# Two engines that stop waiting for their own last instruction, and a 3-tap convolution over two features in turn

## The chip, the cores and the metric

The kernel runs on one core of a Trainium2 chip. Its time is the device time of one execution in microseconds (us), lower is better; 2675.78 us is the median of three executions before the change. The engines named here are TensorE (PE; its weight loads are listed apart as PEld), VectorE (DVE), ScalarE (ACT), GpSimd (POOL) and SyncE (SP), which issues the loads of the weights. Each engine runs its own instructions in order; across engines, and also behind an engine's own earlier instructions, order is kept only by semaphores that an instruction raises when it ends and that another waits for.

## What is computed

One transformer-like block ("block 1") and then two layers of a second kind, on 256 tokens of width 1024, all in fp32. Cut to what matters:

```python
# block 1
h = rms_norm(x) * (1 + scale) + shift;  z = h @ w_in
o = swa_attention(...), rg_lru(conv4(xr)) * gelu(yr), moba_attention(...)     # three branches
x = x + gate * ((sigmoid(g) * (o @ w_branch)).sum() @ w_out)
u = conv3(rms_norm(x) @ w_up);  x = x + gate * ((silu(u_gate) * u_val) @ w_down)   # conv3: 3 taps, per feature
# two layers, each: half FFN, mixer, cross attention to a memory, half FFN
x = x + 0.5 * norm((silu(h @ w1) * (h @ w3)) @ w2)
x = x + norm(merge(conv31(glu), differential attention, pooling) @ w_out)
x = x + norm(cross_attention(x, mem) @ w_o)
```

## The kernel before, in words

Activations lie in SBUF with features on the 128 partitions and the 256 tokens along the free axis, so a feature tile is 128x256 and there are eight of them. Every matrix product runs in fp32 accuracy out of three products of rounded parts: each operand is split into a rounded part ("hi") and the rest ("lo"), and TensorE adds hi*hi, lo*hi and hi*lo. Weights stream from HBM in 704 *units* of up to 512 rows by 256 columns, through six raw buffers. For each unit ScalarE rounds the weights (`hi`, L1099, output `weights_hi`) and VectorE subtracts to get the rest (`lo`, L1421, output `weights_lo`), into a ring of four, three units ahead of TensorE (`pe_unit`, L842). `hi` waits until TensorE has finished the unit that used its ring place before.

The activations are split in the same way: `act_split` (L1170) writes the rounded tile (`h_hi`, `gh`, `mh`), `vec_split` (L1555, L1558) the rest (`h_lo`, `gl`, `ml`). TensorE waits for the split of each feature tile that it reads.

All engines walk one common list of steps, written by `plan`. `spread` mixes chains of small steps (attention heads, the recurrence, the 31-tap convolution) among the gemm units. Steps that the change and the prediction speak of:

- `enter`: four pairs of tiles, each residual add (`vec_residual`, L1574 and L1576, or L1569 in block 1's form), two `act_split`, two `vec_split` and a square (`act_square`, L1144). Between two stages nothing else is there for TensorE.
- attention heads: `pe_scores`, `vec_softmax` (row maxima L1618), `act_softmax` (four exponentials L1218, each followed by a read of the accumulator), `vec_softmax` again (scaling of the probabilities, L1646 and L1648 for the differential form, L1655 otherwise), `pe_turn`, `act_turn` (L1228), `pe_pv`, `vec_pv` (L1664).
- the 31-tap convolution of the mixers: half of the features on VectorE (`vec_conv31`, L1844, three taps a step), half on ScalarE and GpSimd (products `prod` L1359, sums L1973).
- the 3-tap convolution of block 1 (`act_up1`, `vec_up1`): ScalarE writes the last tap of two features, VectorE adds the other two taps of each (L1805).

In the kernel before, nearly every ScalarE and VectorE instruction is followed by a wait of the same engine for that instruction's own semaphore. Only the products L1359 have none. The waits look like this one, in `lo`:

```python
dve.tensor_tensor(WL[s], RAWB[...], WH[s], ALU.subtract).then_inc(sems["weights_rest"], 1)
dve.wait_ge(sems["weights_rest"], up("weights_rest", ("rest", m)))
```

`up` counts the raises of a semaphore and notes the value at which a named result is ready, for the engines that wait for it.

Of the kernel before, what the change touches and what calls it, by code (L numbers as in the profile page):

```python
# [23 lines left out]
P = 128  # L24
# [12 lines left out]
FFN_K = 3  # L37
# [518 lines left out]
def build(nc, a, out, scratch, marks, final, stop=None):  # L556
# [530 lines left out]
    def _(act):  # L1087
# [3 lines left out]
        def hi(m):  # L1091
# [8 lines left out]
            act.wait_ge(sems["weights_rounded"], up("weights_rounded", ("rounded", m)))  # L1100

        def rstd(dst, src, scale, eps, sem, name, s):
# [3 lines left out]
            act.wait_ge(sems[sem], up(sem, name))  # L1106
# [32 lines left out]
        def act_square(k):  # L1139
            p = k["p"]  # L1140
# [5 lines left out]
            act.wait_ge(sems["act_norm"], up("act_norm", ("sq", k["key"], p)))  # L1146
# [6 lines left out]
        def act_adapt(k):  # L1153
            for f in range(NF):
# [4 lines left out]
                act.wait_ge(sems["act_split"], up("act_split", ("split_hi", "H", k["key"], f)))  # L1159

        def act_split(k):
            h = xbuf(k["buf"], k["gen"])[0]
            f = k["f"]
# [7 lines left out]
            act.wait_ge(sems["act_split"], up("act_split", ("split_hi", k["buf"], k["gen"], k["ft0"] + f)))  # L1171

        def act_evac_y(k):
            act.wait_ge(sems["gemm_done"], at("unit", k["last_unit"]))
            ft = k["ft"]
            if k["sq"] is None:
                act.copy(Y[:, ft:ft + 2, :], slot(k["id"])).then_inc(sems["act_drain"], 1)
                act.wait_ge(sems["act_drain"], up("act_drain", ("evac", k["id"])))
# [3 lines left out]
            act.wait_ge(sems["act_drain"], up("act_drain", ("sqy", k["sq"], ft // 2)))  # L1182
            for i in range(2):
                act.activation(Y[:, ft + i, :], slot(k["id"])[:, i, :], ACT.Copy,
                               scale=col(k["gain"][0], k["gain"][1] + ft + i)).then_inc(sems["act_drain"], 1)
                act.wait_ge(sems["act_drain"], up("act_drain", ("evac", k["id"])))
            mark(("y", k["yk"], ft // 2), "act_drain")

        def act_evac_qk(k):
# [5 lines left out]
            act.wait_ge(sems["act_drain"], up("act_drain"))  # L1195
# [9 lines left out]
        def act_evac_v1(k):  # L1205
            act.wait_ge(sems["gemm_done"], at("unit", k["last_unit"]))
            act.copy(BUF[k["dst"]][:, :, k["c0"]:k["c0"] + k["cols"]], GP[:, k["id"] % 2, :, 0:k["cols"]]).then_inc(sems["act_drain"], 1)
            act.wait_ge(sems["act_drain"], up("act_drain", ("evac", k["id"])))
            mark(("tm", k["dst"], 0), "act_drain")

        def act_softmax(k):
            c = att(k["cfg"], k["i"])
            act.wait_ge(sems["vec_attn"], at("max", k["cfg"], k["i"]))
            for qt in range(2):
                nk = P * (qt + 1) if c["causal"] else T
                for m in range(c["maps"]):
                    j = 2 * qt + m
                    act.activation(c["E"][:, qt, m, 0:nk], scores_at(c, qt, m, nk), ACT.Exp, bias=NM[:, j:j + 1], accum_out=DEN[:, j:j + 1]).then_inc(sems["act_attn"], 1)  # L1218
                    act.wait_ge(sems["act_attn"], up("act_attn", ("exps", k["cfg"], k["i"])))
            if k["cfg"] == "swa":  # L1220
                act.activation(ES[:], ES[:], ACT.Exp).then_inc(sems["act_attn"], 1)
                act.wait_ge(sems["act_attn"], up("act_attn", ("sink_exp", k["cfg"], k["i"])))

        def act_turn(k):
# [4 lines left out]
            act.wait_ge(sems["act_attn"], up("act_attn", ("pt", k["cfg"], k["i"], m)))  # L1229

        def act_pv(k):
            if k["cfg"][:4] == "diff":
                act.wait_ge(sems["pe_attn"], at("o_ps", k["cfg"], k["i"]))
                act.activation(ASQ[:, k["i"] // 2 % 2, k["i"] % 2, :], PV[:, 0:T], ACT.Square).then_inc(sems["act_attn"], 1)
                act.wait_ge(sems["act_attn"], up("act_attn", ("o_sq", k["cfg"], k["i"])))
# [8 lines left out]
        def act_evac_xr(k):  # L1244
# [3 lines left out]
            act.wait_ge(sems["act_drain"], up("act_drain", ("evac", k["id"])))  # L1248
            mark(("xr", k["ft"]), "act_drain")

        def act_evac_yr(k):
# [3 lines left out]
            act.wait_ge(sems["act_drain"], up("act_drain"))  # L1255
            act.activation(SQ[:, s, :], slot(k["id"]), ACT.Square).then_inc(sems["act_drain"], 1)
            act.wait_ge(sems["act_drain"], up("act_drain", ("evac", k["id"])))

        def act_gelu(k):
# [3 lines left out]
            act.wait_ge(sems["act_gelu"], up("act_gelu", ("gelu_tanh", k["ft"])))  # L1263

        def act_rnn_gate(k):
# [5 lines left out]
            for g in range(2):  # L1271
                act.activation(o_b1["rg"][:, f % 2, g, :], STAT[:, g * T:(g + 1) * T], ACT.Tanh, scale=0.5,
                               bias=HALFB[:, 8 * g + f:8 * g + f + 1]).then_inc(sems["act_rnn"], 1)
                act.wait_ge(sems["act_rnn"], up("act_rnn", ("stat_read", k["s"])))
            mark(("gate_tanh", "rnn", f), "act_rnn")

        def act_rnn_in(k):
# [4 lines left out]
            act.wait_ge(sems["act_rnn"], up("act_rnn"))  # L1282
# [782 lines left out]
```

## Time and profile before

| | |
|---|---|
| median of three executions | 2675.78 us (2674.79 to 2678.45) |
| the profiled execution, first to last instruction | 2675.4 us |
| TensorE busy | 2407.3 us (90%) |
| VectorE busy | 1800.0 us (67%) |
| ScalarE busy | 1431.5 us (54%) |
| GpSimd busy | 375.0 us (14%) |
| mean granted TensorE clock | 0.942 of full speed |

The profile is one execution; its span agrees with the median within 0.4 us, so sums are made against the span. A busy TensorE is not one at its full pace: the granted clock has two levels, 1.2 and 2.4 GHz, shown as 0.5 and 1.0.

### The profile page before, as it was taken

How to read it: one execution, taken by the hardware profiler on the slowest of the kernel's cores; microseconds unless marked ns; L12 is line 12 of the kernel's file. 1: busy time of each engine (PE TensorE's matmuls, PEld its weight loads, DVE VectorE, ACT ScalarE, POOL GpSimd, SP SyncE). 2: the span in 40 equal slices, each digit the busy share in tenths (PEclk: the TensorE clock that was granted, in tenths of full speed). 3: DMA queues.
4: the chain of work that ended last, by engine and by line, in shares of the span. 5: the costliest groups of instructions: out<-in, count | busy, mean ns of one | idle time of the engine just before them, and what ended most of it. 6: DMA issues, size and time to landing. Idle time of an engine off the chain costs nothing. (4 is left out here: it accounts for less than half of the span.)

```text
span 2675.4 us, 45893 instructions
## 1 busy us (share of the span) xinstructions
PE 2407.3 (90%) x18041; PEld 2291.6 (86%) x18041; DVE 1800.0 (67%) x2425; ACT 1431.5 (54%) x2074; POOL 375.0 (14%) x354
## 2 busy tenths in 40 slices
PE   5988798999998998989898998998998988898997
PEld 5976797999998987878797998998987888797997
DVE  5666886996764886877455664664896877454663
ACT  2564445764445645665635445545644765635443
POOL 1000000110010553420000100010453430000010
PEclk7998998999999998999899999999998999899999
DMA  8534474556654552335343654654452335253652
GB/s 249 147 97 125 149 227 143 175 187 215 182 180 143 157 170 69 118 113 172 104 148 105 189 180 141 175 180 150 143 176 70 115 118 177 94 159 95 189 177 84
DMA packets 402055, 400.52 MB, mean 150 GB/s; under 512 B 18006, under 2 KB 399304, under 8 KB 401841
## 3 DMA queue, kind: packets, MB, share of 16 engines
q1 hardware_dynamic: 399457, 389.27, 47.8%
q0 software_dynamic: 2384, 8.32, 1.1%
q8 instruction: 144, 2.36, 0.4%
q14 instruction: 70, 0.57, 0.1%
HBM read 396.45 MB, written 1.09 MB: 149 GB/s over the span
## 5 line engine op out<-in xcount | busy, mean ns | idle before, releaser
L1421 DVE TENSOR_TENSOR weights_lo<-raw_weights,weights_hi 128x1024 fp32r<-128x1024 f32 x704 | 871.7, 1238 | 471.1 <-ACT weights_hi L1099 457.3
L842 PE MATMUL gemm_ps<-h_hi,weights_hi 128*128 128x256 f32 x3664 | 1074.6, 293 | 98.7 <-DVE h_lo L1555 58.0
L1099 ACT CAST weights_hi<-raw_weights 128x1024 fp32r<-128x1024 f32 x704 | 727.7, 1034 | 617.5 <-PE gemm_ps L842 559.8
L842 PE MATMUL gemm_ps<-h_lo,weights_hi 128*128 128x256 f32 x3664 | 1053.1, 287 | 0.0
L842 PE MATMUL gemm_ps<-h_hi,weights_lo 128*128 128x256 f32 x3664 | 1052.5, 287 | 0.0
L842 PEld LDWEIGHTS gemm_ps<-h_hi,weights_hi 128*128 128x128 f32 x3664 | 720.5, 197 | 115.8 <-issue 89.3
L842 PEld LDWEIGHTS gemm_ps<-h_lo,weights_hi 128*128 128x128 f32 x3664 | 720.8, 197 | 4.1 <-issue 3.0
L842 PEld LDWEIGHTS gemm_ps<-h_hi,weights_lo 128*128 128x128 f32 x3664 | 719.8, 196 | 0.0
L1973 POOL TENSOR_TENSOR y<-y,prod 128x256 f32<-128x256 f32 x240 | 237.3, 989 | 393.5 <-ACT prod L1359 209.8
L1961 POOL TENSOR_TENSOR hidl<-hf,hidh 128x512 fp32r<-128x512 f32 x55 | 73.8, 1342 | 1344.2 <-ACT hidh L1343 1344.2
L842 PE MATMUL gemm_ps<-hidh,weights_hi 128*128 128x256 f32 x880 | 248.2, 282 | 2.0 <-DVE weights_lo L1421 2.0
L842 PE MATMUL gemm_ps<-hidh,weights_lo 128*128 128x256 f32 x880 | 245.7, 279 | 0.0
L842 PE MATMUL gemm_ps<-hidl,weights_hi 128*128 128x256 f32 x880 | 245.5, 279 | 0.0
L842 PE MATMUL gemm_ps<-gh,weights_hi 128*128 128x256 f32 x544 | 165.3, 304 | 34.8 <-DVE gl L1558 19.9
L1844 DVE SCALAR_TENSOR_TENSOR y<-zp,param_cols,y 128x256 f32<-128x256 f32 x240 | 170.2, 709 | 8.5
L842 PEld LDWEIGHTS gemm_ps<-hidh,weights_hi 128*128 128x128 f32 x880 | 165.2, 188 | 2.4 <-DVE weights_lo L1421 2.2
L842 PEld LDWEIGHTS gemm_ps<-hidh,weights_lo 128*128 128x128 f32 x880 | 165.4, 188 | 0.0
L842 PEld LDWEIGHTS gemm_ps<-hidl,weights_hi 128*128 128x128 f32 x880 | 164.7, 187 | 0.2
L842 PE MATMUL gemm_ps<-gl,weights_hi 128*128 128x256 f32 x544 | 157.4, 289 | 0.0
L842 PE MATMUL gemm_ps<-gh,weights_lo 128*128 128x256 f32 x544 | 157.2, 289 | 0.0
L842 PEld LDWEIGHTS gemm_ps<-gh,weights_hi 128*128 128x128 f32 x544 | 108.6, 200 | 39.9 <-issue 32.5
L842 PEld LDWEIGHTS gemm_ps<-gl,weights_hi 128*128 128x128 f32 x544 | 108.4, 199 | 1.4 <-issue 1.0
(282 smaller groups left out, 2926.7 us busy)
## 6 DMA issues: line engine op xcount, KB each, us to landing
raw_weights<-in_ffn_w_dram SPq DMA_DIRECT2D x256, 512.0 KB, 3.9
raw_weights<-in_w_in_dram SPq DMA_DIRECT2D x200, 512.0 KB, 3.8
raw_weights<-in_w_mod_dram SPq DMA_DIRECT2D x48, 512.0 KB, 4.9
raw_weights<-in_w_up_dram SPq DMA_DIRECT2D x44, 512.0 KB, 4.0
raw_weights<-in_xattn_kv_dram SPq DMA_DIRECT2D x32, 512.0 KB, 3.8
raw_weights<-in_w_out_dram SPq DMA_DIRECT2D x24, 512.0 KB, 3.9
raw_weights<-in_w_down_dram SPq DMA_DIRECT2D x20, 512.0 KB, 4.4
raw_weights<-in_w_branch_dram SPq DMA_DIRECT2D x16, 512.0 KB, 4.3
```

The costliest lines, as they stand in the source:

```text
L842: mm = pe.matmul(ps[:, c, 0:T], w[:, m, kt, c * P:(c + 1) * P], x[:, f, :], start=start, stop=stop_)
L1099: act.copy(WH[s], RAWB[:, u["raw"] % RAW, 0:u["nkt"], 0:u["cols"]]).then_inc(sems["weights_rounded"], 1)
L1421: dve.tensor_tensor(WL[s], RAWB[:, u["raw"] % RAW, 0:u["nkt"], 0:u["cols"]], WH[s], ALU.subtract).then_inc(sems["weights_rest"], 1)
L1844: dve.scalar_tensor_tensor(out=Y[:, f, :], in0=o_m["zp"][:, f, j:j + T], scalar=col(f"dw{l}", 8 * j + f), in1=Y[:, f, :], op0=ALU.mult, op ...
L1961: pool.tensor_tensor(l_[:, s, :], src, h[:, s, :], ALU.subtract).then_inc(sems["hidden_rest"], 1)
L1973: pool.tensor_tensor(Y[:, f, :], Y[:, f, :], o_m["prod"][:, b, i, :], ALU.add).then_inc(sems["pool_conv"], 1)
```

## The change

At 69 places the wait of ScalarE or VectorE for its own last instruction is taken out; the raise of the semaphore stays, so other engines wait as before. Where the result is read by the next instruction of the same engine, the wait stays or is set just ahead of the reader. Several waits are put in for readers further on (`vec_qk_norm`, `vec_subln`, `vec_softmax`, `vec_evac_branch`). Two orders are changed: the differential softmax scales the second map of both query tiles before it combines either, and the 3-tap convolution runs tap by tap over two features instead of feature by feature. `vec_conv31`, `vec_mod`, `vec_rnn_conv`, `vec_rnn_mult`, `vec_rnn_scan` and the set-up keep their waits. No instruction that computes is added, removed or changed in size. The core of the diff (the places left out replace `wait_ge(sems[s], up(s, name))` by `up(s, name)` in the same way):

```diff
         def hi(m):
...
             act.copy(WH[s], RAWB[:, u["raw"] % RAW, 0:u["nkt"], 0:u["cols"]]).then_inc(sems["weights_rounded"], 1)
-            act.wait_ge(sems["weights_rounded"], up("weights_rounded", ("rounded", m)))
+            up("weights_rounded", ("rounded", m))
...
         def act_split(k):
...
-            act.wait_ge(sems["act_split"], up("act_split", ("split_hi", k["buf"], k["gen"], k["ft0"] + f)))
+            up("act_split", ("split_hi", k["buf"], k["gen"], k["ft0"] + f))
...
         def act_softmax(k):
...
                     act.activation(c["E"][:, qt, m, 0:nk], scores_at(c, qt, m, nk), ACT.Exp, bias=NM[:, j:j + 1], accum_out=DEN[:, j:j + 1]).then_inc(sems["act_attn"], 1)
-                    act.wait_ge(sems["act_attn"], up("act_attn", ("exps", k["cfg"], k["i"])))
+                    up("act_attn", ("exps", k["cfg"], k["i"]))
...
         def lo(m):
...
-            dve.wait_ge(sems["weights_rest"], up("weights_rest", ("rest", m)))
+            up("weights_rest", ("rest", m))
...
         def vec_split(k):
...
-            dve.wait_ge(sems["vec_split"], up("vec_split", ("split", k["buf"], k["gen"], d)))
+            up("vec_split", ("split", k["buf"], k["gen"], d))
...
         def vec_softmax(k):
...
+                second = []
                 for qt in range(2):
                     nk = P * (qt + 1)
                     dve.tensor_scalar(E[:, qt, 1, 0:nk], E[:, qt, 1, 0:nk], RD[:, 2 * qt + 1:2 * qt + 2], None, ALU.mult).then_inc(sems["vec_attn"], 1)
-                    dve.wait_ge(sems["vec_attn"], up("vec_attn"))
+                    second.append(up("vec_attn"))
+                for qt in range(2):
+                    nk = P * (qt + 1)
+                    dve.wait_ge(sems["vec_attn"], second[qt])
                     dve.scalar_tensor_tensor(out=E[:, qt, 0, 0:nk], in0=E[:, qt, 0, 0:nk], scalar=RD[:, 2 * qt:2 * qt + 1], in1=E[:, qt, 1, 0:nk], op0=ALU.mult, op1=ALU.add).then_inc(sems["vec_attn"], 1)
-                    dve.wait_ge(sems["vec_attn"], up("vec_attn", ("probs", k["cfg"], k["i"])))
+                    up("vec_attn", ("probs", k["cfg"], k["i"]))
...
         def vec_up1(k):
...
-            for i in range(2):
-                f = 22 * v + 2 * j + i
-                for n in range(FFN_K - 1):
+            tap = [None, None]
+            for n in range(FFN_K - 1):
+                for i in range(2):
+                    f = 22 * v + 2 * j + i
+                    if n:
+                        dve.wait_ge(sems["vec_ffn"], tap[i])
                     dve.scalar_tensor_tensor(out=uc[:, v, i, :], in0=raw_up[:, v, i, n:n + T],
                                              scalar=col("ffn_conv_w", 44 * n + f), in1=uc[:, v, i, :], op0=ALU.mult,
                                              op1=ALU.add).then_inc(sems["vec_ffn"], 1)
-                    dve.wait_ge(sems["vec_ffn"], up("vec_ffn", ("conv_gate" if v == 0 else "conv_val", j)))
+                    tap[i] = up("vec_ffn", ("conv_gate" if v == 0 else "conv_val", j))
```

## Rows read from the trace of the kernel before

**Rows 1.** The page: busy time by engine; granted TensorE clock in 40 slices.

```profile
PE 2407.3 (90%) x18041; PEld 2291.6 (86%) x18041; DVE 1800.0 (67%) x2425; ACT 1431.5 (54%) x2074; POOL 375.0 (14%) x354
...
PEclk7998998999999998999899999999998999899999
```

**Rows 2.** Waits of TensorE: us in total, times, longest us.

```profile
PE gemm_ps L842 <- DVE h_lo L1555: 58.0, 21, 6.5
...
PE gemm_ps L842 <- DVE gl L1558: 19.9, 2, 10.0
```

**Rows 3.** Waits of the two engines that prepare weights, same columns.

```profile
ACT weights_hi L1099 <- PE gemm_ps L842: 559.8, 359, 4.4
DVE weights_lo L1421 <- ACT weights_hi L1099: 457.3, 328, 7.8
```

**Rows 4.** Stretches: length, busy of PE, PEld, DVE, ACT, POOL, clock, DMA.

```profile
56.00:332.00 276.00, 229.96 (x1559) 204.17 (x1558) 185.13 (x345) 153.75 (x251) 0.89 (x1) 0.91 0.47 137
346.00:413.00 67.00, 63.92 (x536) 62.60 (x535) 58.43 (x93) 33.64 (x50) 0.00 (x0) 1.00 0.77 240
477.00:592.00 115.00, 113.10 (x940) 112.55 (x938) 106.69 (x135) 85.57 (x116) 16.64 (x11) 1.00 0.57 174
668.00:852.00 184.00, 184.00 (x1530) 183.02 (x1528) 109.31 (x110) 88.67 (x102) 14.28 (x11) 1.00 0.60 181
882.00:995.00 113.00, 102.75 (x818) 99.17 (x818) 106.07 (x120) 66.69 (x108) 70.79 (x68) 1.00 0.57 176
1005.00:1175.00 170.00, 144.08 (x949) 127.86 (x949) 135.32 (x200) 113.06 (x216) 69.47 (x69) 0.90 0.31 96
1189.00:1227.00 38.00, 32.77 (x266) 31.78 (x265) 29.21 (x42) 22.77 (x31) 0.00 (x0) 1.00 0.43 133
1264.00:1327.00 63.00, 48.51 (x302) 43.46 (x303) 30.33 (x44) 37.88 (x59) 0.76 (x1) 0.84 0.29 93
```

**Rows 5.** Timeline of ScalarE at 900 us (start, length), and the products' durations in ns.

```profile
899.99 1.05 ACT L1099 CAST weights_hi<-raw_weights 128x1024 fp32r<-128x1024 f32 x1 [1.85 <-PE gemm_ps L842]
901.07 1.31 ACT L1359 ACTIVATE prod<-zp,param_cols 128x256 f32<-128x256 f32 x3
902.29 0.62 ACT L1310 ACTIVATE gt<-gt 128x512 f32<-128x512 f32 x1
...
L1359 ACT ACTIVATE prod<-zp,param_cols x240: 492/498/517, 885.1 to 2174.7; 128x256 f32<-128x256 f32 x120
```

**Rows 6.** Timeline of VectorE in one attention head, and of TensorE behind it.

```profile
1051.73 0.69 DVE L1421 TENSOR_TENSOR weights_lo<-raw_weights,weights_hi 128x512 fp32r<-128x512 f32 x1
1052.46 1.15 DVE L1618 TENSOR_REDUCE neg_max<-misc_ps 128x2 f32<-128x256 f32 x2
1055.96 0.18 DVE L1637 RECIPROCAL rden<-den 128x4 f32<-128x4 f32 x1 [2.35 <-ACT e L1218]
...
1057.53 0.48 DVE L1648 SCALAR_TENSOR_TENSOR e<-e,rden 128x256 f32<-128x256 f32 x1
...
1059.81 0.55 PE L842 MATMUL gemm_ps<-gh,weights_hi 128*128 128x256 f32 x1 [9.99 <-DVE gl L1558]
```

**Rows 7.** Chain that ended last, in an enter: start us, us, what.

```profile
2457.18 0.70 DVE y L1574
...
2458.69 0.52 ACT h_hi L1170
...
2459.30 0.48 DVE h_lo L1555
...
2459.84 0.50 DVE h_lo L1555
...
2460.36 0.70 DVE y L1574
```

**Rows 8.** Groups by line: busy us, mean ns of one, idle before.

```profile
L1844 DVE SCALAR_TENSOR_TENSOR y<-zp,param_cols,y 128x256 f32<-128x256 f32 x240 | 170.2, 709 | 8.5
...
L1555 DVE SCALAR_TENSOR_TENSOR h_lo<-x_res,param_cols,h_hi 128x256 fp32r<-128x256 f32 x64 | 31.0, 484 | 38.3 <-ACT h_hi L1170 36.1 <-DVE h_lo L1555 0.4
```

**Rows 9.** Timeline of VectorE at the 3-tap convolution.

```profile
508.42 1.22 DVE L1421 TENSOR_TENSOR weights_lo<-raw_weights,weights_hi 128x1024 fp32r<-128x1024 f32 x1
509.68 2.05 DVE L1805 SCALAR_TENSOR_TENSOR uc<-up,param_cols,uc 128x256 f32<-128x256 f32 x4
```

More of the change, by code:

```diff
@@ L1105, in rstd @@
             act.activation(dst, dst, ACT.Exp, scale=-0.5).then_inc(sems[sem], 1)
-            act.wait_ge(sems[sem], up(sem, name))
+            up(sem, name)
         def act_setup(k):
@@ L1281, in act_rnn_in @@
             act.activation(o_b1["xr"][:, f, 0:T], s, ACT.Exp, scale=-1.0).then_inc(sems["act_rnn"], 1)
-            act.wait_ge(sems["act_rnn"], up("act_rnn"))
+            up("act_rnn")
             act.activation(o_b1["s_all"][:, f, :], s, ACT.Tanh).then_inc(sems["act_rnn"], 1)
-            act.wait_ge(sems["act_rnn"], up("act_rnn", ("a", f)))
+            up("act_rnn", ("a", f))
         def act_rnn_sqrt(k):
@@ L1545, in vec_adapt @@
                 dve.scalar_tensor_tensor(out=HL[:, f, :], in0=Y[:, f, :], scalar=MODC[:, c:c + 1], in1=HH[:, f, :], op0=ALU.add, op1=ALU.subtract).then_inc(sems["vec_norm"], 1)
-                dve.wait_ge(sems["vec_norm"], up("vec_norm", ("split", "H", k["key"], f)))
+                up("vec_norm", ("split", "H", k["key"], f))
         def vec_split(k):
@@ L1587, in vec_evac_qk @@
             dve.tensor_copy(BUF[k["dst"]][:, k["ft"]:k["ft"] + 2, :], slot(k["id"])).then_inc(sems["vec_drain"], 1)
-            dve.wait_ge(sems["vec_drain"], up("vec_drain", ("evac", k["id"])))
+            up("vec_drain", ("evac", k["id"]))
+            mark(("qk_raw", k["dst"], k["ft"]), "vec_drain")
         def vec_qk_norm(k):
@@ L1622, in vec_softmax @@
                 i = k["i"]
+                dve.wait_ge(sems["vec_attn"], at("max", k["cfg"], k["i"]))
                 for qt in range(2):
@@ L1625, in vec_softmax @@
                     dve.tensor_tensor(NM[:, j], NM[:, j], SINK[:, 2 * i:2 * i + 2], ALU.min).then_inc(sems["vec_attn"], 1)
-                    dve.wait_ge(sems["vec_attn"], up("vec_attn"))
+                    last_min = up("vec_attn")
+                dve.wait_ge(sems["vec_attn"], last_min)
                 for qt in range(2):
@@ L1795, in vec_ffn_val @@
             dve.tensor_tensor(o_f2["hf"][:, b], fa, fb[:], ALU.mult).then_inc(sems["vec_ffn"], 1)
-            dve.wait_ge(sems["vec_ffn"], up("vec_ffn", ("hidden", key, k["j"])))
+            up("vec_ffn", ("hidden", key, k["j"]))
         def vec_up1(k):
@@ L1817, in vec_up1 @@
                                          op0=ALU.mult, op1=ALU.mult).then_inc(sems["vec_ffn"], 1)
-                dve.wait_ge(sems["vec_ffn"], up("vec_ffn", ("hidden", "b1u", j)))
+                up("vec_ffn", ("hidden", "b1u", j))
         def vec_pads2(k):
@@ L1859, in vec_pool_w @@
                 dve.scalar_tensor_tensor(out=o_m["gl2"][:, f, :], in0=slot(k["id"])[:, i, :], scalar=col(f"pscale{l}", f), in1=o_m["gh2"][:, f, :], op0=ALU.mult, op1=ALU.subtract).then_inc(sems["vec_split"], 1)
-                dve.wait_ge(sems["vec_split"], up("vec_split", ("split", "G", f"l{l}mq", f)))
+                up("vec_split", ("split", "G", f"l{l}mq", f))
             mark(("evac", k["id"]), "vec_split")
@@ L1890, in vec_mem_turn @@
                 dve.tensor_copy(o_c["memf"][:, 4 * half:4 * half + 4, :].rearrange("p f t -> p (f t)"), PBF[:, 0:1024]).then_inc(sems["vec_norm"], 1)
-                dve.wait_ge(sems["vec_norm"], up("vec_norm", ("memf", f"l{k['l']}", half)))
+                up("vec_norm", ("memf", f"l{k['l']}", half))
         parts = dict(setup=vec_setup, params=vec_params, turn_x=vec_turn_x, mod=vec_mod, mod_sum=vec_mod_sum, adapt=vec_adapt, split=vec_split,
```

106 lines of the change are left out of this document (54 added, 52 removed).

## The prediction

> **What bounds the kernel now.** I read the page first, then the waits, a table of stretches, and last the timelines of the stretches in which TensorE is idle. TensorE is busy for 2407.3 of 2675.4 us, so 268 us at most lie in its idle time, and its granted clock lies under 0.9 in seven of the 40 slices [rows 1]. It is 1.00 in the stretches where TensorE hardly idles and 0.84 to 0.91 in three of those where it does [rows 4]; what is missing there was granted at the 1.2 GHz level. The waits show for what it is idle: above all for the rests of activations, 58.0 us in 21 waits on one line and 19.9 us in only two on another [rows 2]. The two engines that prepare operands are no bound on average. ScalarE's rounding of weights sat idle 559.8 us until TensorE had freed a ring place, and VectorE's subtraction 457.3 us until the rounding was done [rows 3]: where the weights flow, TensorE sets the pace, and a faster ScalarE or VectorE only waits longer.
>
> The table of stretches separates the two situations. In a feed-forward network TensorE is busy 184.00 of 184 us at the 2.4 GHz level; nothing that the change does can show there. In the mixers, the attention and the merges TensorE lacks 2 to 46 us a stretch, and VectorE is busy for up to 94% (106.07 of 113 us) and 80% (135.32 of 170 us) [rows 4]. There a chain of small VectorE and ScalarE instructions ends last. The gain must come from these chains.
>
> **What one removed wait is worth.** *ScalarE.* The trace has instructions without the wait: three products of 0.498 us each take 1.31 us together instead of 1.49, so each starts 0.09 us before the one ahead has ended, and the tanh behind them, which waits for another engine's finished work, starts at 902.29 while the products run to 902.38. Behind the rounding, which has its own wait, the products start 0.03 us late (901.04 to 901.07) [rows 5]. A removed wait between two ScalarE instructions of which the second is otherwise ready is thus worth 0.09 + 0.03 = 0.12 us.
>
> *VectorE.* Nowhere in this trace do two of its instructions stand without the wait. Known is the gap, 0.04 us (1052.42 to 1052.46), and the fixed part of an instruction: 512 columns take 0.69 us and 1024 take 1.22, so 0.16 us do not depend on the columns [rows 6, 9]. The bounds are 0 (the next one starts no earlier in any case) and 0.16 + 0.035 = 0.19 us (the whole fixed part is hidden). I take 0.11 us, just under ScalarE's value, which is the nearest row.
>
> The Trainium skill's page "VectorE: DVE Perf Modes", section "The DRAIN you can't avoid", speaks against that: each VectorE instruction is followed by a flush, the next cannot start before it, and eight copies took 13.88 us with a semaphore behind each and with one behind the last alone. By that rule the VectorE part of the sum is nothing and the time is that of the first rival below. The section "Two Vector instructions with no wait between them" of the same page says that an instruction whose tensors start in the same partitions as those before it is not held and starts earlier; all tiles here start at partition 0. No row of this trace decides between the two.
>
> **The change part by part.** I followed the chains back along the timelines from each stall of TensorE to the TensorE instruction that had released them, and counted on them the neighbours (gap under 0.06 us) whose wait goes; S is their number on ScalarE, V on VectorE. A stretch cannot gain more than TensorE lacks in it. A wait that stays for a reader costs what it did.
>
> - *Enters* (residual, split). One cycle lasts 3.18 us (2457.18 to 2460.36) and on VectorE holds two freed neighbours: rest to rest, and rest to the next product [rows 7]. Residual to rounding goes over to ScalarE and keeps its price. V = 7 an enter, 0.77 us, seven enters: 5.4 us. Block 1's form has V = 11: 1.2 us. Sum 6.6.
> - *Conv31 with the gated inputs.* Only the weights' rest ahead of three taps, and the gates, are freed; the taps keep their waits. S = 7, V = 42: 5.4 us of 10.2 that TensorE lacks [rows 4]; two layers: 10.9.
> - *Differential attention and the merge behind it.* In the head shown, TensorE idles 9.99 us behind a chain that runs through two maxima, four exponentials, four scalings and the rest [rows 6]. Freed on it: one neighbour of the maxima, three of the exponentials, three of the scalings (their new order leaves each pair independent), four around them. Over the stretch S = 33, V = 67: 11.4 us of 26 [rows 4]; two layers: 22.7.
> - *Last merge of the mixer.* S = 1, V = 29: 3.3 us of 5.2 [rows 4]; two layers: 6.6.
> - *Memory and cross attention.* S = 20, V = 7: 3.2 us of 14.5 [rows 4]; two layers: 6.3.
> - *Block 1.* Up to 332 us S = 51, V = 60: 12.7 us of 46. The merge (346 to 413) and the feed-forward network with the 3-tap convolution (477 to 592) have long chains, but TensorE lacks only 3.1 and 1.9 us there, which is all that they can give [rows 4]. The four taps now take 2.05 us [rows 9]; tap by tap they have three freed neighbours and take about 1.7, at 44 steps behind a TensorE that is busy 98%, so the new order is worth nearly nothing. With 0.9 us in the second adaptive norm: 18.6.
> - *Output.* V = 3: 0.3.
> - *Weights elsewhere, feed-forward networks of the layers, the waits put in for later readers.* Nothing: TensorE covers them [rows 3, 4]; the new waits are for results that are several instructions old. If that cover failed, each would cost a gap of 0.04 us.
>
> Nothing is moved past a DMA queue: SP issues a load when the weights' rest has been taken, as before, and POOL's list is untouched.
>
> The sum is 6.6 + 10.9 + 22.7 + 6.6 + 6.3 + 18.6 + 0.3 = 72 us if nothing else is right behind each chain. Something often is: 376 of 704 rests of weights found their rounding already done, 328 waited for it [rows 3], so close to half of what VectorE gains is met by another wait. Between 0.53 (376/704) and 1 I take 0.65, nearer to the low end because TensorE itself paces the roundings. 72 x 0.65 = 47 us: 2675.4 - 47 = 2628 us, and with the 0.4 us by which the median lies above the span, **2629 us**. Time regained at the 2.4 GHz level is inside the counts, as the lacks include slow matmuls only in part; I add nothing for it.
>
> **Rivals.**
>
> 1. *VectorE regains nothing, ScalarE all of its own.* The S terms alone: in block 1 51 x 0.12 = 6.1, in its merge S = 8 or 1.0, and the 1.9 that its feed-forward network can give; in the layers 7, 33, 1 and 20 neighbours or 0.8 + 4.0 + 0.1 + 2.4, twice; 23.6 us; by 0.65 that is 15: 2660 us. For it: no row shows VectorE overlapping. Against it: it has a fixed part much like ScalarE's, which does. Chance 0.21; 2650 to 2669.
> 2. *The gain is hidden.* TensorE's own progress releases the chains (559.8 us of the roundings' idle [rows 3]), and each stall is only shifted to the next wait: within 0.2%, 5.4 us, which is about what a measurement of this kernel can tell: 2675 us. Against it: the 9.99 us stall has no TensorE work in it at all [rows 6]. Chance 0.11.
> 3. *Slower: VectorE and GpSimd collide more.* The taps of conv31 take 0.709 us where the same form elsewhere takes 0.484 [rows 8], in stretches in which GpSimd is busy 70.79 of 113 us [rows 4]: 0.225 x 240 = 54 us are lost to that already, and VectorE is the bound there. If the gaps between VectorE's instructions are what lets GpSimd through, an addition would meet two of them instead of one, and twice the collision costs 54 us more: 2629 + 54 = 2683 us. It decides from 47/240 = 0.2 us more a tap. Against it: the taps keep their waits and so their gaps. Chance 0.06.
> 4. *More than forecast.* All 72 us arrive (2604 us), or VectorE also hides its whole fixed part, 0.08 us more at some 420 neighbours, 34 us (2570 us). For it: the chains of the mixers have few other waits. Chance 0.10 for below 2602.
>
> **How the numbers follow.** The forecast itself, both engines overlapping and part of the gain lost, has 0.52 and goes from 2602 to 2650. The range leaves out the slower rival, the half of the hidden one that lies above 2672, and what lies below 2595 (0.06 + 0.06 + 0.07): 2595 to 2672. Faster by over 0.2% are the forecast, the first and the fourth rival, 0.83; within 0.2% is the second, 0.11; slower 0.06.
>
> **What would show it.** Right: ScalarE's neighbours start 0.09 us before the one ahead of them ends, and two rests in a row on VectorE take about 0.93 us instead of the 1.04 from 2459.30 to 2460.34 [rows 7]; an enter's cycle falls from 3.18 to about 2.95; the 9.99 us stall to about 8.8; VectorE's busy time falls by 80 us or more, ScalarE's by over 60, TensorE's stays near 2407, and the feed-forward stretches keep their length. Two rests still at 1.04 mean the first rival; shorter pairs with equal stretches the second; taps above 0.71 us the third. The prediction is wrong above all if VectorE's value is far from 0.11 or if the share of 0.65 is.

## The result, and the profile after

The changed kernel takes 2549.46 us (median of four runs, 2549.18 to 2552.1) against 2675.78 before: ratio 0.9533, 95% interval 0.9522 to 0.9545, 126 us less. The forecast was 2629 us, 47 us less, with 2595 as the lower end. The direction was right, the size was not. The profiled execution has a span of 2547.5 us.

The page of the changed kernel, busy time by engine and granted clock, answers to [rows 1]:

```profile
PE 2365.3 (93%) x18041; PEld 2265.1 (89%) x18041; DVE 1721.2 (68%) x2425; ACT 1323.8 (52%) x2074; POOL 387.5 (15%) x354
...
PEclk9998999999999998999999999999998999999998
```

TensorE's idle time fell from 268 to 182 us and its busy time from 2407.3 to 2365.3, so of the 128 us between the spans 86 were stalls and 42 a shorter busy time of the same 18041 matmuls. Its waits and those of the two preparing engines, answering to [rows 2, 3]:

```profile
PE gemm_ps L842 <- DVE h_lo L1555: 45.4, 17, 5.8
PE gemm_ps L842 <- DVE gl L1558: 14.7, 2, 7.3
```

```profile
ACT weights_hi L1099 <- PE gemm_ps L842: 612.0, 386, 4.8
DVE weights_lo L1421 <- ACT weights_hi L1099: 463.5, 358, 7.8
```

The stretches of [rows 4] between about the same roundings of weights (first column start:end, then length, busy of PE, PEld, DVE, ACT, POOL, clock):

```profile
633.00:816.00 183.00, 183.00 (x1523) 182.27 (x1522) 106.34 (x109) 82.61 (x100) 14.30 (x11) 1.00 0.61 182
54.00:309.00 255.00, 229.10 (x1567) 203.83 (x1565) 173.95 (x346) 137.66 (x251) 0.89 (x1) 0.92 0.51 148
844.00:953.00 109.00, 103.38 (x821) 100.63 (x819) 102.27 (x118) 63.69 (x108) 72.98 (x68) 0.98 0.59 179
960.00:1115.00 155.00, 138.83 (x948) 123.68 (x946) 127.20 (x198) 101.33 (x216) 75.81 (x70) 0.93 0.35 106
1198.00:1252.00 54.00, 44.47 (x307) 40.64 (x307) 28.26 (x45) 33.74 (x61) 0.76 (x1) 0.96 0.34 109
```

The feed-forward stretch keeps its length; the others are 4 to 21 us shorter. A cycle of an enter, on the timeline (start, length, what), answers to [rows 7]:

```profile
2332.24 0.91 ACT L1170 ACTIVATE h_hi<-x_res,param_cols 128x256 fp32r<-128x256 f32 x2 [1.36 <-DVE x_res L1576]
...
2333.58 0.68 DVE L1574 TENSOR_TENSOR y<-y,rstd_y 128x512 f32<-128x512 f32 x1
2334.30 0.69 DVE L1576 SCALAR_TENSOR_TENSOR x_res<-y,x_res 128x512 f32<-128x512 f32 x1
2335.02 0.91 ACT L1170 ACTIVATE h_hi<-x_res,param_cols 128x256 fp32r<-128x256 f32 x2 [1.36 <-DVE x_res L1576]
2335.57 0.88 DVE L1555 SCALAR_TENSOR_TENSOR h_lo<-x_res,param_cols,h_hi 128x256 fp32r<-128x256 f32 x2 [0.58 <-ACT h_hi L1170]
```

From `h_hi` to `h_hi`, 2332.24 to 2335.02, the cycle is 2.78 us, where 3.18 stood. Two rests of 0.48 us take 0.88: the second starts 0.08 us before the first has ended, where it started 0.04 after. Two roundings of 0.51 take 0.91. And there is something that the prediction did not look for: the rounding starts 0.03 us behind the residual's end (2334.30 + 0.69 = 2334.99, then 2335.02), where it started 0.09 behind it before (2457.91 + 0.69 = 2458.60, then 2458.69):

```profile
2457.91 0.69 DVE L1576 SCALAR_TENSOR_TENSOR x_res<-y,x_res 128x512 f32<-128x512 f32 x1
2458.69 1.05 ACT L1170 ACTIVATE h_hi<-x_res,param_cols 128x256 fp32r<-128x256 f32 x2 [1.46 <-DVE x_res L1576]
```

The attention head of [rows 6], VectorE and TensorE behind it:

```profile
1006.10 1.01 DVE L1620 TENSOR_REDUCE neg_max<-misc_ps 128x2 f32<-128x256 f32 x2
1008.90 0.18 DVE L1641 RECIPROCAL rden<-den 128x4 f32<-128x4 f32 x1 [1.79 <-ACT e L1218]
```

```profile
1011.99 0.55 PE L842 MATMUL gemm_ps<-gh,weights_hi 128*128 128x256 f32 x1 [7.34 <-DVE gl L1558]
```

The stall is 7.34 us instead of 9.99; about 8.8 was forecast. The wait for the four exponentials alone is 1.79 instead of 2.35.

Last, the group of the table load ahead of the logarithm in `rstd` (xcount, busy us, mean ns, idle before it), first of the kernel before, then of the changed one (with the logarithm that follows), and last ScalarE's timeline at one of them after the change:

```profile
L1103 ACT ACT_TABLE_LOAD x37 | 47.5, 1283 | 55.1 <-PE misc_ps L913 37.9 <-PE misc_ps L939 6.5 <-PE misc_ps L1046 4.3
```

```profile
L1103 ACT ACT_TABLE_LOAD x37 | 47.5, 1283 | 0.7
...
L1103 ACT ACTIVATE rstd_x<-misc_ps,eps 128x256 f32<-128x256 f32 x10 | 4.8, 476 | 20.4 <-PE misc_ps L913 20.3
```

```profile
2338.36 1.28 ACT L1103 ACT_TABLE_LOAD   x1
2342.22 0.48 ACT L1103 ACTIVATE rstd_x<-misc_ps,eps 128x256 f32<-128x256 f32 x1 [2.58 <-PE misc_ps L913]
```

Before, ScalarE sat idle for TensorE's sum and then loaded the table for 1.28 us; now the load runs while TensorE still adds. Nothing in the diff speaks of that load.

### The profile page after: what moved, and what is told of

It is laid out like the page before. It is cut to its first block, busy times and chain, and to the rows that moved or that the text cites. A ratio compares the mean times of both kernels' runs of the same rounds, so it can differ in the third digit from the quotient of the medians.

```text
span 2547.5 us, 44221 instructions
## 1 busy us (share of the span) xinstructions
PE 2365.3 (93%) x18041; PEld 2265.1 (89%) x18041; DVE 1721.2 (68%) x2425; ACT 1323.8 (52%) x2074; POOL 387.5 (15%) x354
## 4 chain that ended last, share of the span: by engine, by line
PE 75%; DVE 15%; ACT 6%; issue 4%; DMA 1%; ACTq 0%; POOL 0%; DVEq 0%; POOLq 0%
PE gemm_ps L842 62%; DVE weights_lo L1421 4%; PE gemm_ps L845 3%; DVE y L1857 3%; PE misc_ps L970 2%; PE misc_ps L969 2%; PE misc_ps L913 2%; ACT L1103 1%; ACT weights_hi L1099 1%; DVE y L1574 1%; DVE x_res L1576 1%; DVE mod_partial L1518 1%; ACT h_hi L1170 1%; PE misc_ps L1002 1%; ACT e L1218 1%
## 5 line engine op out<-in xcount | busy, mean ns | idle before, releaser
L1421 DVE TENSOR_TENSOR weights_lo<-raw_weights,weights_hi 128x1024 fp32r<-128x1024 f32 x704 | 859.2, 1230 | 467.0 <-ACT weights_hi L1099 463.5
L842 PE MATMUL gemm_ps<-h_hi,weights_hi 128*128 128x256 f32 x3664 | 1068.0, 291 | 68.1 <-DVE h_lo L1555 45.4
L1099 ACT CAST weights_hi<-raw_weights 128x1024 fp32r<-128x1024 f32 x704 | 718.6, 1031 | 664.2 <-PE gemm_ps L842 612.0
L1986 POOL TENSOR_TENSOR y<-y,prod 128x256 f32<-128x256 f32 x240 | 249.3, 1039 | 352.4 <-ACT prod L1359 197.0
L1857 DVE SCALAR_TENSOR_TENSOR y<-zp,param_cols,y 128x256 f32<-128x256 f32 x240 | 187.2, 780 | 5.7
L1359 ACT ACTIVATE prod<-zp,param_cols 128x256 f32<-128x256 f32 x240 | 104.8, 505 | 3.2 <-POOL y L1986 3.2
```

The source lines that it names most:

```text
L842: mm = pe.matmul(ps[:, c, 0:T], w[:, m, kt, c * P:(c + 1) * P], x[:, f, :], start=start, stop=stop_)
L1099: act.copy(WH[s], RAWB[:, u["raw"] % RAW, 0:u["nkt"], 0:u["cols"]]).then_inc(sems["weights_rounded"], 1)
L1359: act.activation(o_m["prod"][:, b, i, :], o_m["zp"][:, f, j:j + T], ACT.Copy, scale=col(f"dw{k['l']}", 8 * j + f)).then_inc(sems["act_prod ...
L1421: dve.tensor_tensor(WL[s], RAWB[:, u["raw"] % RAW, 0:u["nkt"], 0:u["cols"]], WH[s], ALU.subtract).then_inc(sems["weights_rest"], 1)
L1857: dve.scalar_tensor_tensor(out=Y[:, f, :], in0=o_m["zp"][:, f, j:j + T], scalar=col(f"dw{l}", 8 * j + f), in1=Y[:, f, :], op0=ALU.mult, op ...
L1986: pool.tensor_tensor(Y[:, f, :], Y[:, f, :], o_m["prod"][:, b, i, :], ALU.add).then_inc(sems["pool_conv"], 1)
```

## The experiments

Three theories stood after the comparison: neighbours on one engine, that is, two instructions in a row, overlap (O); the table load left the path (L); TensorE's clock fell less often (C). A fourth came after the first four runs, when the starts behind other engines' instructions were measured: an instruction that waits for another engine starts sooner (H). Each run below is compared with the kernel before on the same chip, whose medians were 2673 to 2676 us.

**Each engine alone.** ScalarE's or VectorE's program is taken from the changed kernel, all else from the kernel before.

> The kernel before with the changed kernel's ScalarE program alone; VectorE waits for itself as before. The whole change gained 126.3 us (2675.8 to 2549.5). Theory (both engines regain about 0.1 us of overlap for each wait, and ScalarE's program also lets the table load ahead of Ln run before its statistic is there): about 70 us of it here, 2605 us, of which up to 25 are the table loads; anything from 2590 to 2625 fits. Rival A (VectorE regains nothing, since it drains after each instruction anyway): nearly the whole gain is here, 2550 to 2565 us. Rival B (ScalarE is hidden, VectorE is what the chains wait for): 2650 us or more.

> The kernel before with the changed kernel's VectorE program alone (with its two new orders); ScalarE waits for itself as before, and all its table loads stay behind the statistic. Theory: about 45 us gained, 2630 us (2615 to 2645), since 1030 VectorE instructions of the changed kernel start 40 to 130 ns before the end of the one ahead where none did before. Rival A (VectorE regains nothing): 2675 us. If the two engines' gains simply add, this one and the run with ScalarE alone make 126 us together; if each hides behind the other, less.

ScalarE alone: 2624.9 us, ratio 0.9819 (0.9804 to 0.9833). VectorE alone: 2612.3 us, 0.9772 (0.9758 to 0.9787). So VectorE regains time, and more than ScalarE. In its trace some 980 VectorE instructions start on average about 83 ns before the one ahead has ended, and none did before. ScalarE alone lies at the upper end of what was expected for it, VectorE alone 3 us under its range. The two gains, 49 and 62, make 110 of 126. The 16 that are missing can lie in the table loads, which are worth more once both engines' chains are short (next runs), or in one engine's gain that meets the other's waits; these two runs do not tell which.

**The table load.** In the changed kernel the load is put back behind the statistic; in the kernel before it is brought ahead, with all own waits kept and only their order changed.

```diff
 # changed kernel; the same in the other three callers of rstd
         def act_rstd(k):
+            act.wait_ge(sems["weights_rounded"], count["weights_rounded"])
             act.wait_ge(sems["pe_norm"], at("stat", k["s"]))
```

> The changed kernel with one more wait, always met, ahead of the statistic's wait in the four callers of rstd, so that the wait for TensorE's statistic stands ahead of the table load again (37 times) and nothing else changes. Theory: the 1.28 us load comes back onto the path where the statistic came late: 15 to 25 us slower than the changed kernel, 2565 to 2575 us; in the trace the idle time ahead of the L1103-type load comes back to about 50 us. Rival (the loads were hidden, the gain is overlap alone): within 4 us of the changed kernel, 2549 to 2554 us.

> The kernel before with all its own waits kept, and only their order changed ahead of Ln: the wait for TensorE's statistic comes first and the own wait last, so that the table load no longer waits for the statistic. Theory: 15 to 25 us faster than before, 2651 to 2661 us. Rival (the loads are hidden by other work of TensorE): 2674 to 2677 us.

For the second of the two the own wait is held back and written behind the statistic's. Pinned: 2571.7 us, 22 above the changed kernel, and the idle time ahead of the load is back at 60.0 us. Ahead in the old kernel: 2662.3 us, 0.9957 (0.9940 to 0.9974), 11.5 us less, under the 15 to 25 that were expected. L is real, and worth about twice as much once the chains around it are short. The group's rows, pinned and then ahead:

```profile
L1103 ACT ACT_TABLE_LOAD x37 | 47.5, 1283 | 60.0 <-PE misc_ps L913 39.6 <-issue 7.4 <-PE misc_ps L1046 5.0
```

```profile
L1125 ACT ACT_TABLE_LOAD x37 | 47.5, 1283 | 2.9
...
L1125 ACT ACTIVATE rstd_x<-misc_ps,eps 128x256 f32<-128x256 f32 x10 | 4.8, 477 | 14.6 <-PE misc_ps L913 14.5
```

**The handoff.** Where an instruction waited for itself and for another engine, the latter stood ahead. In the records the start came 102 ns (median of some 450) behind ScalarE's instruction on VectorE and 94 ns (some 110) behind VectorE's on ScalarE; after the change 32 ns (some 490) and 35 ns (some 100). The first run turns the order round in the kernel before on both engines; the second and third put a wait that was met long ago first in the changed kernel, with and without the loads pinned.

```diff
 # kernel before, one of the places: `own` holds the wait back and writes it last
-            act.wait_ge(sems["weights_rounded"], up("weights_rounded", ("rounded", m)))
+            act.own(sems["weights_rounded"], up("weights_rounded", ("rounded", m)))
 # changed kernel: at an instruction's first wait, if it is for another engine
+                    engine.wait_ge(sems["act_setup"], 1)
                 engine.wait_ge(sem, v)
```

> The kernel before with every own wait kept; only the order of an instruction's waits is turned round on ScalarE and VectorE: the other engine's result first, the own last instruction last. No instruction may overlap the one ahead of it, so overlap cannot gain. Theory: before the change an instruction that two waits held started 102 ns (ScalarE to VectorE) and 94 ns (VectorE to ScalarE) behind the other engine's instruction, and 32 and 35 ns in the changed kernel, because the wait that stands alone ahead of the instruction costs time after it is met and the wait that the instruction itself carries does not. Then this kernel has the short handoffs too, and the early table loads: 35 to 60 us below before, 2614 to 2639 us. Rival (the gain is overlap, the handoff is not on the chains): the early table loads alone, as measured, 2660 to 2664 us.

> The changed kernel with one more wait, on a value long met, put first at every ScalarE and VectorE instruction that waits for another engine and not for its own: nothing waits longer for data, and neighbours still overlap, but each such instruction has two waits again and its handoff the old length, and the table load stands behind the statistic. Theory: 30 to 55 us slower than the changed kernel with the loads pinned (2571.7), so 2600 to 2625 us. Rival (only overlap and the loads count): 2570 to 2575 us.

> The changed kernel with the second, long met wait put first wherever ScalarE or VectorE waits for another engine, except ahead of Ln, so that the table loads stay early: only the handoffs are long again (102 instead of 32 ns from ScalarE to VectorE). If the handoffs are worth what the kernel with pinned loads and two waits lost beside the one with pinned loads alone (11 us): 2557 to 2564 us. Rival (that difference was not the handoffs): 2549 to 2552 us.

The first miss: 2703.6 us, 1.0107 (1.0092 to 1.0122), slower than before. Its handoffs are short, but the own wait now stands ahead and is the one met last wherever two neighbours follow each other:

```profile
2479.75 0.69 DVE L1606 TENSOR_TENSOR y<-y,rstd_y 128x512 f32<-128x512 f32 x1
2480.48 0.69 DVE L1608 SCALAR_TENSOR_TENSOR x_res<-y,x_res 128x512 f32<-128x512 f32 x1
2481.21 1.13 ACT L1186 ACTIVATE h_hi<-x_res,param_cols 128x256 fp32r<-128x256 f32 x2 [1.38 <-DVE x_res L1608]
2481.75 1.11 DVE L1587 SCALAR_TENSOR_TENSOR h_lo<-x_res,param_cols,h_hi 128x256 fp32r<-128x256 f32 x2 [0.58 <-ACT h_hi L1186]
2482.43 0.63 ACT L1160 ACTIVATE squares<-x_res 128x512 f32<-128x512 f32 x1
2482.99 0.69 DVE L1606 TENSOR_TENSOR y<-y,rstd_y 128x512 f32<-128x512 f32 x1
```

The rounding starts 0.04 us behind the residual, as in the changed kernel, but two rests take 1.11 us instead of 1.04, and the cycle 3.24 instead of 3.18. Of VectorE's neighbours about 1080 now have a gap of 111 ns on average, where about 1820 had 35. The expectation had overlooked that. A lone wait that is met last costs about 60 to 75 ns in either case, whether it is for another engine or for the engine itself.

With a second wait and pinned loads: 2582.9 us (0.9659, 0.9642 to 0.9675), 11 above the pinned kernel; with the loads early: 2561.7 us (0.9580, 0.9565 to 0.9594), 12 above the changed kernel, as expected of it. H is worth about 12 us, not the 30 to 55 that the run with pinned loads was expected to show. That run keeps neither the early loads nor the short handoffs, and is still 92 us faster than the kernel before: that is what O, with the two new orders and all that follows from it, is worth. In the enter of the first of the two, neighbours overlap (0.91 and 0.88) and the handoffs are long; the cycle is 2.91 us:

```profile
2357.60 0.69 DVE L1608 TENSOR_TENSOR y<-y,rstd_y 128x512 f32<-128x512 f32 x1
2358.32 0.69 DVE L1610 SCALAR_TENSOR_TENSOR x_res<-y,x_res 128x512 f32<-128x512 f32 x1
2359.10 0.91 ACT L1187 ACTIVATE h_hi<-x_res,param_cols 128x256 fp32r<-128x256 f32 x2 [1.48 <-issue]
2359.71 0.88 DVE L1589 SCALAR_TENSOR_TENSOR h_lo<-x_res,param_cols,h_hi 128x256 fp32r<-128x256 f32 x2 [0.70 <-ACT h_hi L1187]
...
2360.51 0.68 DVE L1608 TENSOR_TENSOR y<-y,rstd_y 128x512 f32<-128x512 f32 x1
```

**The removed waits in five groups.** Functions of the changed kernel are put one group at a time into the kernel before, each time with the loads kept behind the statistic; the five together are all removed waits but the one at the end of `rstd`. The first group, as an example:

```diff
-            act.wait_ge(sems["weights_rounded"], up("weights_rounded", ("rounded", m)))
+            up("weights_rounded", ("rounded", m))
...
-            dve.wait_ge(sems["weights_rest"], up("weights_rest", ("rest", m)))
+            up("weights_rest", ("rest", m))
```

> The kernel before with only the waits behind the weights' rounding and behind the weights' rest removed, and all table loads kept behind the statistic. The prediction put these at nothing outside the convolution: TensorE covers them. If so: 2670 to 2676 us. Theory of the handoff: what follows a rounding or a rest on its engine, in the stretches where a chain ends last, is released by one wait instead of two and starts earlier too: 10 to 20 us, 2655 to 2665 us.

> The kernel before with only the enters' own waits removed (residual, squares, roundings and rests of activations, the adaptive norm), table loads kept behind the statistic. The prediction's term was 6.6 us, 4.3 after its share of 0.65: 2667 to 2671 us. Theory now (rows of the changed kernel put an enter's cycle at 2.79 instead of 3.18 us, four cycles, seven enters; half of the cycle's gain belongs here and half to the handoffs): 10 to 18 us, 2656 to 2664 us.

> The kernel before with only the attention functions' own waits removed on both engines (maxima, exponentials, scalings, copies of the turned probabilities, q and k norms, outputs), table loads kept. Were each group's gain passed on in full, the four groups (this one, enters, convolution with gates, the rest) and the weights' 27 us would make the 102 us that the changed kernel keeps with its loads pinned, and this one about 25 us: 2649 us. If each group alone loses part of its gain to the waits that are still there, as the prediction's share of 0.65 supposed: 10 to 17 us, 2657 to 2664 us.

> The kernel before with only the own waits of the gated inputs, the merges, the pooled branch and the convolution's norm removed. Passed on in full, about 25 us: 2649 us. With the prediction's share: 10 to 17 us, 2657 to 2664 us.

> The kernel before with only the remaining own waits removed: evacuations of the outputs, block 1's recurrent branch and gelu, the feed-forward networks with the 3-tap convolution in its new order (3.6 us by itself). Passed on in full about 20 us: 2654 us; with the prediction's share 10 to 14 us: 2660 to 2664 us.

> The kernel before with only the 3-tap convolution's function replaced: the taps of two features in turn, each waiting for its own feature's last tap. The prediction: nearly nothing, since TensorE is busy for 98% of that stretch: 2671 to 2676 us. Rival (the chain of taps holds TensorE up): 44 steps of about 0.35 us less, up to 15 us, 2660 us.

```
group                    us       ratio (95% interval)       less than before, us
weights                  2647.6   0.9905 (0.9886 to 0.9924)  27.2
enters                   2652.1   0.9916 (0.9901 to 0.9931)  21.0
attention                2643.6   0.9882 (0.9857 to 0.9908)  29.5
convolution, gates       2664.6   0.9968 (0.9955 to 0.9981)   8.4
rest (with tap order)    2664.3   0.9961 (0.9946 to 0.9976)   8.7
tap order alone          2671.2   0.9985 (0.9975 to 0.9994)   3.6
```

The five make 94.8 us; the changed kernel with pinned loads has 102.1, and the 7 between them are within the intervals. Nothing like a third is lost by a group alone to the own waits that the others still have. What chains lose to waits that the change leaves in place, these runs do not show. Weights, enters and attention gave more than was expected of each alone; the convolution with the gates and the rest gave less than either of their two forecasts, of which the higher was only a share of what remained. The tap order alone kept within the prediction's "nearly nothing". The weights gain nothing where TensorE covers them (2 of their 27 us lie in the feed-forward networks and output products, 1196 us long), and the rest where chains pass through them.

**The clock.** Matmuls that nobody reads fill TensorE's longest stalls in the changed kernel.

```diff
             ps = GP[:, u["pair"] % 2, :, :]
+            for _ in range(FILL.get(u["m"], 0)):          # 12 to 62, in 13 units
+                pe.matmul(ps[:, 0, 0:T], WH[:, m, 0, 0:P], WL[:, m, 0, 0:T], start=True, stop=True)
```

> The changed kernel with matmuls that nobody reads put into TensorE's longest stalls (in 13 units ahead of the wait for the first rest, 12 to 62 of them, into the accumulator that the unit then starts afresh; and 9 ahead of the first scores of each differential attention), so that TensorE does not idle there. They leave out nothing and wait for nothing new. Theory (the clock falls to 1.2 GHz around a stall and costs time in the dense matmuls behind it): a higher mean granted clock than 0.966, and 5 to 15 us faster, 2535 to 2545 us, mostly behind the two long stalls ahead of the pooled branch and behind the scores. Rival (the 42 us less TensorE busy time came with the chains, the clock is only a symptom): within 3 us of the changed kernel.

2549.2 us, 0.9535 (0.9520 to 0.9549): no difference, where 5 to 15 us had been expected. The page shows 552 more matmuls, and fewer slices under the full clock; the mean went from 0.966 to 0.980:

```profile
PE 2411.2 (95%) x18593; PEld 2313.8 (91%) x18593; DVE 1720.8 (68%) x2425; ACT 1323.9 (52%) x2074; POOL 388.4 (15%) x354
...
PEclk9998999999999999999999999999999999999998
```

The stalls left in 11 of the 13 units show that the filling did not take back what the clock gave: there TensorE started the unit's own work 0.04 us behind VectorE's rest, with the filling over 0.06 to 0.40 us earlier. In the other two units and ahead of the scores the filling ran past the operands, so there a gain could be hidden by it. TensorE's waits for the rests of activations, 45.4 us in the changed kernel, are still 21.1 with the filling:

```profile
PE gemm_ps L846 <- DVE h_lo L1561: 21.1, 19, 1.8
```

So C is not a cause in those 11 stalls: TensorE was waiting for the chain anyway. Whether the clock was worth something in the other stalls, or in the longer ones of the kernel before, was not tried.

**A version beyond the change.** The 31-tap convolution's taps on VectorE, left alone by the change, are taken from two features in turn, the second 15 taps behind, so that no tap waits for the one ahead; alone, and with the filled stalls. The last run also writes the wait that ends last first, at instructions with two foreign waits.

```diff
-            for j in range(1 + k["part"] * CONV_TAPS, 1 + (k["part"] + 1) * CONV_TAPS):
+            for f, j in order[n:n + CONV_TAPS]:           # (0,1) .. (0,15), (0,16), (2,1), (0,17), (2,2), ...
...
-                dve.wait_ge(sems["vec_conv"], up("vec_conv", ("conv", l)))
+                tap[l, f] = up("vec_conv", ("conv", l))   # waited for by this feature's next tap
```

> The changed kernel, and in addition the 240 taps of the 31-tap convolution that VectorE does are taken from two features in turn, the second one 15 taps behind the first, each waiting for the tap two instructions back: the same work, no tap waits for the one ahead of it. Theory (each neighbour is worth the 0.117 us that the traces show, and the chain behind the taps gets all of it): 240 x 0.117 = 28 us less VectorE time, in stretches where TensorE still lacks some 45 us in all; 10 to 25 us faster than the changed kernel, 2525 to 2540 us. Rival (the slower one of the prediction's: without gaps on VectorE the collisions with GpSimd grow): taps well above 0.78 us, 2550 us or more.

> Both of the two kernels ahead of this together. Theory: their gains add, 2515 to 2535 us. Rival: the taps in turn shift the stalls, so that the filling matmuls hold TensorE up: slower than the better of the two.

> The kernel with the taps in turn (2539 us), and where an instruction waits for two other engines, the wait that ends last in the trace is written first, so that the instruction itself carries it: the weights' rounding (TensorE's release before the load), TensorE's units (the first rest before the weights' rest), the turn of the probabilities (the output's copy before the probabilities) and the output's copy. Theory: TensorE starts 45 to 90 ns sooner behind some 40 of VectorE's results: 2 to 6 us faster, 2533 to 2537 us. Rival: no difference, 2538 to 2542 us.

Taps in turn: 2539.3 us, 0.9501 (0.9487 to 0.9515), 10 us below the changed kernel and the first version that beats both; that is the low end of the 10 to 25 that were expected. With filled stalls 2542.4 us, 0.9506 (0.9490 to 0.9522), no better, where 2515 to 2535 had been expected. With the late wait first 2538.0 us, 0.9492 (0.9476 to 0.9508), no difference that can be told. Taps and GpSimd's additions by line, in the changed kernel and then with the taps in turn:

```profile
L1857 DVE SCALAR_TENSOR_TENSOR y<-zp,param_cols,y 128x256 f32<-128x256 f32 x240 | 187.2, 780 | 5.7
...
L1986 POOL TENSOR_TENSOR y<-y,prod 128x256 f32<-128x256 f32 x240 | 249.3, 1039 | 352.4 <-ACT prod L1359 197.0 <-issue 134.9 <-POOL y L1986 5.5
```

```profile
L1877 DVE SCALAR_TENSOR_TENSOR y<-zp,param_cols,y 128x256 f32<-128x256 f32 x240 | 184.2, 806 | 1.4
...
L2006 POOL TENSOR_TENSOR y<-y,prod 128x256 f32<-128x256 f32 x240 | 254.7, 1061 | 339.0 <-ACT prod L1366 196.2 <-issue 116.9 <-POOL y L2006 10.7
```

## Why the prediction was wrong

The 126 us are about 22 of table loads, 12 of handoffs and 92 of neighbours and what follows from them. The forecast had 47, all of them neighbours: 72 before its share. So of the 79 us that it lacked 25 are the share, 20 more neighbours or a higher price, 22 the loads and 12 the handoffs. Between the starts of the same roundings of weights in the two traces the gains in us are as follows (first column of numbers: the prediction's sum before its share, its enters put where they lie; the columns sum to 72, 128 and 106 us of span):

```
stretch, both layers               predicted   changed   loads pinned
block 1 up to its network            17.9        31.4       28.4
network with the 3-tap convolution    1.9         2.1        2.1
conv31 and gated inputs              10.9        15.9       15.9
differential attention, merge        22.7        32.6       23.3
last merge of the mixer               6.6         8.1        8.0
memory and cross attention            7.8        20.1       13.2
networks, output products, enters     4.2        17.7       15.1
```

- *What bounds the kernel, and where nothing can show*: right. The feed-forward stretches kept their length, the mixers, attentions and merges gave the time.
- *Price of a neighbour*: right, both a little low. ScalarE 0.12 forecast, 0.105 + 0.030 = 0.135 us in the records; VectorE 0.11 forecast, 0.082 + 0.035 = 0.117. VectorE's busy time fell by 79 us (80 forecast). The first rival, VectorE regaining nothing, fell with the run of VectorE's program alone. The rule of the Trainium skill behind it ("VectorE: DVE Perf Modes", section "The DRAIN you can't avoid"), by which the next instruction cannot start before the flush, does not describe these instructions: they start 0.08 us early. The section "Two Vector instructions with no wait between them" of that page, by which only a held instruction must wait for all earlier ones to finish, agrees with that.
- *The share of 0.65*: this step failed. It was read from how often the weights' rest waits for its rounding, and 237 of those 328 waits lie outside block 1's first stretch, the mixers and the attentions. On the chains that count no such loss shows: with the loads pinned every stretch of the table gained at least the sum before the share (12 us of handoffs are in that column), and the five groups alone make 93% of what they make together. Without the share the prediction stands at 72 us, 2604 us, its own fourth rival. Since the counts were also too low (below), a smaller loss cannot be ruled out.
- *"A wait that stays for a reader costs what it did", and the residual to rounding that "keeps its price"*: failed. Taking one of two waits away made each handoff some 60 to 70 ns shorter, about 12 us in all. This, and chains that were not followed, made the enters' term too small: 6.6 forecast, 21.0 measured for those functions alone, which also split operands outside the enters. The forecast cycle was 2.95, the measured one 2.78; with the handoffs long again it is 2.91.
- *The table loads*: missing from the prediction, which had no term for them and gave no reason: 22 us. The 55.1 us of idle time ahead of the load stood in the groups of the trace, under a line that the diff hardly touches.
- *TensorE's busy time "stays near 2407"*: wrong, it fell by 42 us, with a mean granted clock of 0.966 instead of 0.942; that no separate gain was added for the clock was right as far as the filled stalls can tell.
- *The order of the taps worth nearly nothing*: 3.6 us, nearly right. *Hidden gain* (second rival): fell. *Collisions with GpSimd* (third rival): they grew, 0.709 to 0.780 us a tap [rows 8], 17 us of VectorE's time, far from the 0.2 us a tap at which that would decide. The trace shows what they meet: in the changed kernel the 135 taps during most of which (over 80%) GpSimd is busy take 0.91 us on average, the 65 during which it is idle 0.48; before, 108 and 82 taps took 0.88 and 0.49. So about half of the growth is that more taps met GpSimd, and the rest that those that met it took longer. With the taps in turn they grow to 0.806, and about 196 more neighbours overlap instead of 240, part of why the 28 us less waiting that were expected gave 10.

With the measured prices the prediction's counts make 78 us of the 92. The other 14 lie in neighbours that it did not count, or in what a shorter chain gives beyond its own length; the runs do not tell which.
